# Column sums by split products in a two-layer decoder kernel, with the steps around them reordered

## What is computed

```python
# layer 0, retention, per head of 4 (DK 256, DV 512)
q, k = rotary(q), rotary(k) * DK ** -0.5
scores = (q @ k.T) * decay                # inside a chunk
o = scores @ v + (q @ S) * q_dec          # own part and carried state S
S_new = exp(C * lg) * S + (k * k_dec).T @ v
o = rmsnorm(o, gn_w)                      # needs the sum of o*o over 512 values
x = x + (o * silu(g)) @ w_out
# shared K/V and layer 1, block-sparse attention
k, v = split(rmsnorm(x, kv_norm_w) @ w_kv)   # needs the sum of x*x over 1024 values
q = rmsnorm(q.reshape(T, 8, 128), q_norm_w)  # a norm for each token and head
s = q @ k_cached.T + bias                    # 16 cached pages of 128 keys
```

## Time and profile before

| what | value |
|---|---|
| three runs, median | 517.38 us |
| the profiled execution, its own time | 517.27 us |
| its span, first to last instruction | 515.5 us |
| PE busy | 509.7 us, 99% |
| DVE, ACT, POOL busy | 345.9, 259.3, 73.0 us |
| granted clock of TensorE, mean | 1.000 of 2.4 GHz |
| moved by DMA | 125.50 MB, mean 243 GB/s |

### The profile page before, as it was taken

The page is one execution under the profiler, slowest core; times in us unless marked ns, Lnnn a source line. Parts: engine busy times, 40 slices in busy tenths (PEclk is TensorE's granted clock), DMA queues, the critical chain, the costliest instruction groups (busy, mean ns, idle before and its releaser), DMA issues.

```text
span 515.5 us, 9427 instructions
## 1 busy us (share of the span) xinstructions
PE 509.7 (99%) x3550; PEld 439.6 (85%) x3550; DVE 345.9 (67%) x639; ACT 259.3 (50%) x520; POOL 73.0 (14%) x82
## 2 busy tenths in 40 slices
PE   8999999999999999999999999999999999999997
PEld 6989977899779977898899999988877778999885
DVE  3855448892878838883599967845857664776662
ACT  5835542582328532472552546664535655555540
POOL 0291005420091104420000130100000000000000
PEclk9999999999999999999999999999999999999999
DMA  9993969999999999979927967425696747784211
GB/s 270 315 352 107 275 247 342 387 304 218 317 353 344 222 270 318 371 258 227 264 87 279 337 217 270 161 98 199 235 351 213 259 129 240 238 307 172 83 51 51
DMA packets 79232, 125.50 MB, mean 243 GB/s; under 512 B 3907, under 2 KB 42004, under 8 KB 79060
## 3 DMA queue, kind: packets, MB, share of 16 engines
q1 hardware_dynamic: 79106, 124.89, 75.2%
q10 hardware_dynamic: 82, 0.02, 0.0%
HBM read 98.93 MB, written 27.57 MB: 245 GB/s over the span
## 4 chain that ended last, share of the span: by engine, by line
PE 96%; ACT 1%; DVE 1%; issue 1%; DMA 0%; POOL 0%; DVEq 0%; POOLq 0%
PE bank L865 45%; PE bank L862 20%; PE bank L847 7%; PE bank L1028 3%; PE bank L969 3%; PE bank L1042 2%; PE bank L1095 1%; PE bank L987 1%; PE bank L941 1%; PE bank L928 1%; PE bank L1141 1%; PE bank L881 1%; PE bank L974 1%; PE bank L955 1%; PE bank L956 1%; PE bank L954 1%
## 5 line engine op out<-in xcount | busy, mean ns | idle before, releaser
L1498 DVE TENSOR_TENSOR w_lo<-w_raw,w_hi 128x512 fp32r<-128x512 f32 x207 | 145.0, 738 | 69.5 <-ACT w_hi L1165 69.2
L1165 ACT ACTIVATE w_hi<-w_raw 128x512 fp32r<-128x512 f32 x208 | 118.4, 619 | 47.6 <-PE bank L865 22.5
L865 PE MATMUL bank<-xn_hi,w_hi 128*128 128x320 f32 x320 | 100.6, 318 | 0.6 <-ACT w_hi L1165 0.6
L865 PE MATMUL bank<-xn_hi,w_lo 128*128 128x320 f32 x320 | 97.6, 309 | 0.0
L865 PE MATMUL bank<-xn_lo,w_hi 128*128 128x320 f32 x320 | 97.5, 309 | 0.0
L862 PE MATMUL bank<-w_hi,xn_hi 128*128 128x512 f32 x160 | 65.0, 406 | 0.0
L865 PEld LDWEIGHTS bank<-xn_hi,w_hi 128*128 128x128 f32 x320 | 59.7, 188 | 4.4 <-issue 2.5
L862 PE MATMUL bank<-w_lo,xn_hi 128*128 128x512 f32 x160 | 62.6, 392 | 0.0
L862 PE MATMUL bank<-w_hi,xn_lo 128*128 128x512 f32 x160 | 62.5, 390 | 0.0
L865 PE MATMUL bank<-ym_hi,w_hi 128*128 128x320 f32 x192 | 61.5, 320 | 0.0
L865 PEld LDWEIGHTS bank<-xn_lo,w_hi 128*128 128x128 f32 x320 | 59.8, 188 | 0.5
(11 more groups left out here) (248 smaller groups left out, 740.1 us busy)
## 6 DMA issues: line engine op xcount, KB each, us to landing
w_raw<-in_ret_w_in SPq DMA_DIRECT2D x23, 1024.0 KB, 10.9
st<-in_state_ret SPq DMA_DIRECT2D x32, 512.0 KB, 8.0
out_ret_state_sample<-st SPq DMA_DIRECT2D x32, 512.0 KB, 4.6
w_raw<-in_ret_w_out SPq DMA_DIRECT2D x8, 1024.0 KB, 9.3
w_raw<-in_moba_w_in SPq DMA_DIRECT2D x8, 1024.0 KB, 6.3
cache<-in_cache_k SPq DMA_DIRECT2D x16, 512.0 KB, 4.8
w_raw<-in_w_kv SPq DMA_DIRECT2D x8, 1024.0 KB, 6.2
cache<-in_cache_v SPq DMA_DIRECT2D x16, 512.0 KB, 5.2
```

What stands on the lines that cost most here:

```text
L865: mm = pe.matmul(bank[out][:, 0:T], w[:, wk, P * tile:P * tile + P], x[:, k, :], **flags)
L1165: act.activation(w_hi[:, c % 2, part], w_raw[:, c % RAW, part], ACT.Copy).then_inc(w_hi_done, 1)
L1498: dve.tensor_tensor(w_lo[:, c % 2, part], w_raw[:, c % RAW, part], w_hi[:, c % 2, part].bitcast(F32), ALU.subtract).then_inc(w_lo_done, 1)
```

## The change

Six edits go together:

1. The sums SS and NS become two fp32r products of 320 columns with ones in fp32r, of a hi and a lo half of the summed squares. Two steps make the halves: SP (per head) and NA (residual).
2. The residual's squares are added first: GpSimd and VectorE add all eight, and one NS step takes the place of five. It stands in the second tile of mq; RMS and ME 0 move to that tile's end.
3. In OP the first value tile is multiplied as three fp32r products with `sT_hi` and `sT_lo`; the second stays fp32.
4. The sample scores by values go ahead of the states, as two fp32r products over 128 partitions, which hold the hi and the lo values; XC h,0 and XC h,1 stand in one gap.
5. The four one-column sums of QS become four products with 128 columns; a third transpose in QT replaces the separate roots.
6. KS takes two pages at once, 256 keys a product.

```diff
     def states(h):
-        return [[], [("XC", h, 0), ("UP", h, 0)], [("UP", h, 1)], [("XC", h, 1), ("UP", h, 2)], [("UP", h, 3)], [],
-                [("FX", h), ("GNA", h), ("SG", h)], [("US", h)], [("SS", h)], [("SR", h), ("SM", h)]]
+        return [[], [("XC", h, 0), ("XC", h, 1), ("UP", h, 0)], [("UP", h, 1)], [("UP", h, 2)], [("UP", h, 3)], [],
+                [("FX", h), ("GNA", h), ("SG", h)], [("US", h), ("SP", h)], [("SS", h)], [("SR", h), ("SM", h)]]
...
-    for at, step in ((0, ("XC", 3, 0)), (1, ("SH", 2)), (2, ("XC", 3, 1)), (4, ("FX", 3)), (4, ("GNA", 3)), (5, ("SG", 3)),
-                     (6, ("SS", 3)), (8, ("SR", 3)), (9, ("SM", 3)), (11, ("SH", 3)), (13, ("UP", 3, 0)), (16, ("UP", 3, 1)),
+    for at, step in ((0, ("XC", 3, 0)), (0, ("XC", 3, 1)), (1, ("SH", 2)), (4, ("FX", 3)), (4, ("GNA", 3)), (5, ("SG", 3)),
+                     (5, ("SP", 3)), (7, ("SS", 3)), (9, ("SR", 3)), (10, ("SM", 3)), (12, ("SH", 3)), (13, ("UP", 3, 0)), (16, ("UP", 3, 1)),
...
-        if n % 2:
-            g[20 + 2 * n].append(("NS", n))
-    g[31].append(("NS", KT - 2))
+    g[31].append(("NA", 0))
...
-    mid = [[("NS", KT - 1)]] + [[("ME", n)] + ([("QS", 0)] if n == 5 else []) for n in range(MH - 1)]
-    end = [[("RMS",)]] + [[] for _ in range(MH - 1)]
+    mid = [[("NA", 1)], [("NS",)]] + [[("ME", n)] + ([("QS", 0)] if n == 5 else []) for n in range(1, MH - 1)]
+    end = [[], [("RMS",), ("ME", 0)]] + [[] for _ in range(MH - 2)]
...
# TensorE
                 elif kind == "NS":
-                    mm = pe.matmul(bank[5][:, 0:T], ones, scr[:, kt, :], start=kt == 1, stop=kt == KT - 1)
+                    pe.wait_ge(sum_lo_done, RH + 1)
+                    await_free(pe, 5, "NORM", 1)
+                    pe.matmul(bank[5][:, 0:T], ones_r[:, :], sums_hi, start=True, stop=False)
+                    close(pe.matmul(bank[5][:, 0:T], ones_r[:, :], sums_lo, start=False, stop=True), 5)
...
                 elif kind == "OP":
+                    pe.wait_ge(vp_hi_done, h + 1)
+                    pe.wait_ge(vp_lo_done, 2 * h + 1)
+                    pe.wait_ge(sT_hi_done, h + 1)
+                    pe.wait_ge(sT_lo_done, h + 1)
...
-                        pe.matmul(o, vp[:, 0, P * e:P * e + P], sT[:, 0:TP], start=True, stop=False)
-                        mm = pe.matmul(o[:, P:TP], vp[:, 1, P * e:P * e + P], sT[:, TP:TP + P], start=False, stop=True)
+                        pe.matmul(o, vp_hi[:, 0, at], sT_hi[:, :], start=True, stop=False)
+                        pe.matmul(o, vp_hi[:, 0, at], sT_lo[:, :], start=False, stop=False)
+                        pe.matmul(o, vp_lo[:, 0, at], sT_hi[:, :], start=False, stop=False)
+                        mm = pe.matmul(o[:, P:TP], vp[:, 1, at], sT_own[:, :], start=False, stop=True)
...
                 elif kind == "XC":
+                        pe.wait_ge(vs_lo_done, h + 1)
+                        pe.wait_ge(s2_lo_done, h + 1)
+                        pe.matmul(bank[5][:, :], s2_hi[:, :], vs_split[:, :], start=True, stop=False, skip_group_check=True)
+                        pe.matmul(bank[5][:, :], s2_lo[:, :], vs_split[:, :], start=False, stop=False, skip_group_check=True)
...
-                        for j in range(4):
-                            pe.matmul(bank[5][32 * j:32 * j + 32, :], s2[:, 32 * j:32 * j + 32], vs[:, :], start=False, stop=False)
...
                 elif kind == "SS":
-                    pe.wait_ge(sq_sum_done, step[1] + 1)
+                    pe.wait_ge(sum_lo_done, step[1] + 1)
...
-                    close(pe.matmul(bank[5][:, 0:T], ones, scr[:, 4, :], start=True, stop=True), 5)
+                    pe.matmul(bank[5][:, 0:T], ones_r[:, :], sums_hi, start=True, stop=False)
+                    close(pe.matmul(bank[5][:, 0:T], ones_r[:, :], sums_lo, start=False, stop=True), 5)
...
-                            mm = pe.matmul(bank[5][:, TP + pair:TP + pair + 1], flat_sqs[:, P * pair:P * pair + P], ones[:, 0:1],
+                            mm = pe.matmul(bank[5][32 * pair:32 * pair + 32, TP:TP + P], pick[:, 1:33], flat_sqs[:, P * pair:P * pair + P],
...
-                            mm = pe.matmul(bank[5][32 * j:32 * j + 32, cols], window(2 * h + b // 4, b % 4), ktc[:, n % 2, h, :],
+                            mm = pe.matmul(bank[5][32 * j:32 * j + 32, PAST * half_at:PAST * half_at + PAST],
+                                           window(2 * h + b // 4, b % 4), ktc[:, :, h, :],
...
# ScalarE: SC gains sT_hi and two copies to s2_hi, and
+                elif kind == "SP":
+                    act.wait_ge(sq_sum_done, h + 1)
+                    act.activation(sums_hi, scr[:, 4, :], ACT.Copy).then_inc(sum_hi_done, 1)
+                elif kind == "NA" and step[1] == 1:
+                    act.wait_ge(sq_sum_done, RH + 1)
+                    act.activation(sums_hi, scr[:, 7, :], ACT.Copy).then_inc(sum_hi_done, 1)
...
# VectorE: SC gains sT_lo and takes the first vp_lo from OP, OP gains s2_lo, and
+                elif kind == "SP":
+                    dve.wait_ge(sum_hi_done, step[1] + 1)
+                    dve.tensor_tensor(sums_lo, scr[:, 4, :], sums_hi.bitcast(F32), ALU.subtract).then_inc(sum_lo_done, 1)
+                elif kind == "NA" and step[1] == 0:
+                    dve.wait_ge(pair_sum_done, 5)
+                    dve.wait_ge(sq_done, RH + KT - 1)
+                    done(dve.tensor_tensor(scr[:, 6, :], scr[:, 6, :], scr[:, 5, :], ALU.add))
+                elif kind == "NA":
+                    done.wait()
+                    dve.wait_ge(sq_done, RH + KT)
+                    dve.tensor_tensor(scr[:, 7, :], scr[:, 7, :], scr[:, 6, :], ALU.add).then_inc(sq_sum_done, 1)
+                    dve.wait_ge(sum_hi_done, RH + 1)
+                    dve.tensor_tensor(sums_lo, scr[:, 7, :], sums_hi.bitcast(F32), ALU.subtract).then_inc(sum_lo_done, 1)
```

More of the change, by code:

```diff
@@ L181, in add @@
             fill(5, "UR", s[1])
-        if s[0] == "KS" and s[1] % 8 == 0:
-            fill(5, "PS", s[1] // 8)
+        if s[0] == "KS" and s[1] % 4 == 0:
+            fill(5, "PS", s[1] // 4)
         if s[0] == "KP":
@@ L319, in build @@
         scr_split = sb("scr_split", [P, KT * T], F32R)
-        eye = sb("eye", [P, 2 * P + 4])
-        ident, ones, own = eye[:, 0:P], eye[:, P:2 * P], eye[:, 2 * P:2 * P + 4]
+        eye = sb("eye", [P, P + 4])
+        plain = ExitStack()
+        ones = sb("ones", [P, P], F32, plain)
+        plain.close()
+        ones_r = sb("ones_r", [P, P], F32R)
+        sums_hi, sums_lo = (scr_split[:, n * T:n * T + T] for n in (5, 6))
+        ident, own = eye[:, 0:P], eye[:, P:P + 4]
         wcols = sb("wcols", [P, 48])
@@ L1017, in _ @@
                     await_free(pe, 7, *step)
-                    for t in range(2):
+                    for t in range(3):
                         mm = pe.transpose(bank[7][:, P * t:P * t + P], q_rows[:, P * t:P * t + P], ident)
@@ L1375, in _ @@
                     act.activation(kd_hi, kd[:, :, :], ACT.Copy).then_inc(kd_hi_done, 1)
+                    await_read(act, 5, *step)
+                    for at in (0, TS):
+                        act.activation(s2_hi[at:at + TS, :], s2[:, :], ACT.Copy).then_inc(s2_hi_done, 1)
                 elif kind == "OP":
@@ L1866, in _ @@
             pool.memset(eps[:, 1:2], EPS * HD).then_inc(eps_done, 1)
+            pool.wait_ge(eps_done, 1)
+            pool.memset(s2_lo[TS:P, :].bitcast(F32), 0.0).then_inc(s2_lo_cleared, 1)
+            pool.wait_ge(s2_lo_cleared, 1)
             cos, sin = cst[:, C_COS:C_COS + T], cst[:, C_SIN:C_SIN + T]
@@ L1910, in _ @@
                     pool.wait_ge(sq_done, RH + kt + 1)
[L1911 removed]
+                    for n in range(1, 3 if kt > 1 else 2):
+                        if n == 2:
+                            pool.wait_ge(pair_sum_done, kt - 1)
+                        pool.tensor_tensor(scr[:, kt, :], scr[:, kt, :], scr[:, kt - n, :], ALU.add).then_inc(pair_sum_done, 1)
                 elif kind == "MB":
```

122 lines of the change are left out of this document (66 added, 56 removed).

## The result

The changed kernel takes **523.95 us** (median of 4 executions, 523.29 to 525.28) against 517.2 for the kernel before: a ratio of 1.0134, with a 95% interval of 1.0118 to 1.0151. It is slower, as forecast, but by 6.8 us and not by the 2.2 of the forecast's sum (10.2 - 8.0), and it lies outside the range (513.6 to 523.0). The profiled execution took 523.85 us with a span of 522.1.

What follows compares the result with a forecast made beforehand. TensorE, busy for 99% of the span, was taken to bound the kernel: 517.27 less 8.0 of savings plus 10.2 of new waits gives 519.5, or 519.6 us for the median. The eight-in-ten range was 513.6 to 523.0.

Steps and rivals of the forecast that it cites:

- The second term on the path of the heads' sums: Heads 0 to 2: later GpSimd rotations fall on VectorE's additions ahead of SS; 1.5 us, bounds 0 and 3.1.
- The prediction's 8.0: TensorE's summed savings in SS, NS, scores by values, XC, OP, QS and QT: 8.0 us, between 6.1 and 8.8.
- The chain of the residual's sum: Later NS delays root, reciprocal and ME 0, so TensorE waits for w_lo by mk 0: 2.0 us, bounds 1.2 and 2.3.
- Nothing regains it: SS of heads 0 to 2: TensorE, without idle time, waits 2.0 us a head for sums_lo, 5.9 in three.
- The waits are covered: Rival: VectorE is ahead at SS of heads 0 to 2, only head 3 and mk 0 cost; 512.2 us, chance 0.13.
- half of the waits: Rival: no contention, and mk 0's chain regains some lateness or two other waits are shorter; 515.9 us, chance 0.18.
- The port is a lock: Rival: additions and first SG operations in heads 0 to 2 wait out whole rotations; 524.6 or 522 us, chance 0.13.
- Not what they seem: Rival: fp32r products of 256 columns in OP cost 0.147 and joining XC gains nothing; 521.5 us, chance 0.10.
- the cover of OP: OP's wait for sT_lo and the first vp_lo, costed at nothing: about 0.9 us left in head 1.

Runs made afterwards that it cites:

- both moves: Changed kernel with the heads' sums' split directly behind the additions and the residual's sum as two plain fp32 products at mq 0's first half: 515.5 us.
- the last run: Kernel with plain sums (511.7 us), second addition of squares in heads 0 to 2 behind the gate product and all following w_lo: 521.9 us.

## Why the prediction was wrong

Two terms of the sum failed. The second term on the path of the heads' sums was put at 1.5 us and came to about twice that; and a fall of the granted clock behind the new waits, 3.1 us in the profiled execution, was put at nothing. Without the falls the time would have been about 520.8 us, inside the range.

**Right: what TensorE saves.** With plain sums the span from the first projection to the end is 499.25 us against 505.24, 6.0 less. The prediction's 8.0, less the 1.0 of the heads' sums and the 0.8 by which two plain sums cost more than two fp32r ones in the residual, is 6.2. Term by term: a residual pair takes 0.29 (two starts 0.147 apart), an OP block 0.58, the key scores nothing less. Scores by values take 0.56 and not 0.46, as they pay the switch to the column tiles that the states' product paid before.

**Right: where TensorE waits.** Every wait stands at the place, and for the buffer, that the prediction named: 2.3, 3.15 and 3.1 us in heads 0 to 2, 0.64 in head 3, 1.6 for `w_lo` in mq 3 and mk 0. The chain of the residual's sum was 2.0 by the forecast. By the marks, the part behind head 3's SF got 1.08 us shorter; it had 4.0 of savings (the forecast's own) and some 0.9 of head 3's wait in it, which leaves 2.0.

**Wrong, in size: the second term on that path.** "Bounds 0 and 3.1; I take the middle, 1.5." The run with the join undone shows 3.1 us less of wait. The kind of cost and its direction came from the earlier trace rows and stood; the middle was no estimate, and the three heads were not alike. Against the projection product ahead of the sum, the first rotation starts 0.3, 2.1 and 3.8 us later than before in heads 0, 1 and 2, not 1.9 in each; why head 0 moved so little is open. The forecast had most of the term in heads 0 and 1 and least in head 2; the additions and SG grew by 0.67, 1.83 and 1.83 us. The Trainium skill (SBUF — State Buffer, section SBUF: two separate sides) says that the shared pair of ports is an exclusive lock, and the rows agree with it. In all traces of this study together, 38 additions of 640 columns began under an operation of GpSimd, and each ended 0.68 or 0.69 us behind the end of that operation; 19 of 320 columns ended 0.35 behind it; and 33 rotations that began under an addition ended 0.73 to 0.76 behind the addition's end. So each engine sits out what is left of the other's current operation, and the two take turns for as long as the rotations last: that can be counted from rows, operation by operation.

**Wrong, and the larger part: "Nothing regains it", the price of a wait at its own length.** A wait of TensorE costs the length in its row, some 0.3 us beside it, and, at times, a spell at the lower clock. The heads show all three. By the forecast's savings (0.24 + 0.54 + 0.15 + 0.27 = 1.20) a head without waits is 58.98 - 1.20 = 57.8 us; the plain sums give the same, 58.05 - 0.24. Head 2 (184.75 to 245.91) has 61.16: 3.11 of wait and 0.3. Head 0 has 61.88: 2.30, 0.3 and 1.5; head 1 has 62.75: 3.15, 0.3 and 1.5. So the three heads lost 8.6 + 0.9 + 3.1 us against 7.4 in the forecast.

The error closes, to a few tenths. Forecast 519.5 for the profiled execution, less 0.85 of start-up, plus 2.1 for the waits and what stands beside them, plus 3.1 for the clock: 523.85, as measured; that it closes to the hundredth is luck. In head 2 the clock stayed up, and in the other executions it fell once, twice and three times, so the size of this term was chance, between one and three times 1.5 us.

**The range was also narrower than its own bounds.** Savings of at least 6.1 and waits of at most 12.6 give 517.27 - 6.1 + 12.6 = 523.8, not 523; and the waits' four upper bounds add up to 12.1 (5.9 + 3.1 + 0.8 + 2.3).

**Rivals.** "The waits are covered" and "half of the waits" did not occur. "The port is a lock" had the mechanism right and its size wrong: it counted whole operations, 2.5, 2.5 and 1.5 us in the heads, and the rows have 0.67, 1.83 and 1.83. That its 522 to 524.6 hold the result is luck, since the clock made up the rest. "Not what they seem" is out, by the rows of OP.

**Also missed: the cover of OP.** "Costed at nothing ... about 0.9 us are left" held in the changed kernel, but only because its heads had grown by 3 us of wait. Once the split was moved up, VectorE was late for OP and for the `w_lo` ahead of it, by 1.1 us in head 1. In none of the orders that were tried did three heads take less than the 176.95 us of before (178.4 with the early split, 178.8 with both moves, 180.3 with the split behind SG, one fall of the clock in it, and 180.6 with `w_lo` held back); only taking the split sums out gave the time back (174.16).

## What to carry to other kernels

In this kernel, splitting an operand to spare the bottleneck engine a slow product put a chain of two more engines ahead of it. A saving of 0.24 us was not worth a remainder that stands behind 3 us of other work in that engine's order, and it was best left plain. Before moving work to a helper engine, count its backlog at the place where the bottleneck engine comes for it. Where two bounds of a contention are far apart, count the overlap, operation by operation, instead of taking the middle. And put more than its length on a wait of TensorE.

## What the runs showed of the hardware that I had not expected

- The granted clock of TensorE can fall from 2.4 to 1.2 GHz behind a short wait. In each of the six falls profiled here it stayed down for 3.4 us, at a cost of about 1.5 us, and it fell between 0.3 us ahead of the wait's end and 1.4 us behind it. It fell with waits of 1.85, 2.28, 2.30, 2.64, 3.15 and 3.19 us, and it stayed up behind others of 1.89, 1.94, 1.98, 2.48, 2.64, 3.11, 3.15, 3.24 and 3.26. Behind the waits of under 1.8 us that were profiled here (1.75 the longest) it never fell, but one execution that was not profiled, of a kernel with no longer waits than these, has the mean clock of one fall. What decides is open: it is not the kind of product, and among these not the length; the same kernel had none, two or three falls in different executions. The moment at which a wait comes was not varied by itself.
- So kernels with such waits scatter more, and the mean clock sorts their times: 520.2 to 520.6 us without a fall, 523.2 with two and 524.2 to 524.8 with three in the last run. Not all scatter is of this kind: the kernel with plain sums, which has no such wait, took 511.0 to 514.0 us at 0.999 and 1.000.
- VectorE beside GpSimd, both reading SBUF: an addition of 640 columns took up to 1.50 us instead of 0.83, one of 320 columns 1.06 instead of 0.49, and rotations of 320 columns 1.12 to 1.47 instead of 0.88. Each sat out the rest of the other engine's operation (ends 0.68, 0.35 and 0.74 us behind it). VectorE's scaling of a gate tile, which reads one operand from a bank of PSUM, was not held up: 0.47 to 0.49 us in all 61 cases that began under an operation of GpSimd, as in the 195 that did not.
